# Inner feed-forward units: the low-part product of each weight tile right behind its high-part product

## The reference

```python
def swiglu(h, w_gate, w_up, w_down):
    return (jax.nn.silu(h @ w_gate) * (h @ w_up)) @ w_down
...
for i in range(DEPTH):
    g = norm_gain[i]
    h = swiglu(rmsnorm(x, g[0]), ffn_w_gate[i, 0], ffn_w_up[i, 0], ffn_w_down[i, 0])
    x = x + MACARON_WEIGHT * rmsnorm(h, g[1])
    ...
    h = swiglu(rmsnorm(x, g[4]), ffn_w_gate[i, 1], ffn_w_up[i, 1], ffn_w_down[i, 1])
    x = x + MACARON_WEIGHT * rmsnorm(h, g[5])
```

## Time and profile before

| | us |
|---|---|
| median of 3 runs (1092.91 to 1094.5) | 1093.01 |
| span of the profiled execution | 1091.1 |
| TensorE matmuls busy | 1081.5 (99%) |
| TensorE weight loads busy | 947.5 (87%) |
| VectorE busy | 810.8 (74%) |
| ScalarE busy | 662.7 (61%) |
| lines 1922 and 1928 busy | 287.9 and 160.7 |

### The profile page before, as it was taken

One profiled execution on the slowest core, in us unless ns is written; L12 is line 12 of the kernel. 1 busy time (PEld: TensorE's weight loads), 2 busy tenths in 40 slices (PEclk: granted clock), 3 DMA queues, 4 the chain that ended last, 5 costly groups with the idle time before them and its releaser, 6 DMA issues. The chain is left out here.

```text
span 1091.1 us, 17376 instructions
## 1 busy us (share of the span) xinstructions
PE 1081.5 (99%) x6271; PEld 947.5 (87%) x6271; DVE 810.8 (74%) x1230; ACT 662.7 (61%) x1002; POOL 64.0 (6%) x85
## 2 busy tenths in 40 slices
PE   9999999999999999999999999999999999999997
PEld 7888888899888888888888888899999988888886
DVE  5867666786688666668776667899999998766663
ACT  7555455784685455457554556687777797554552
POOL 3000000000010000000000000142111111000000
PEclk9999999999999999999999999999999999999999
DMA  9865645375356654555646534585544537656521
GB/s 285 307 225 165 208 155 153 102 234 187 118 184 234 217 192 156 191 193 184 223 161 222 189 119 135 184 268 186 176 154 154 167 116 237 223 165 230 173 96 39
DMA packets 162882, 199.29 MB, mean 183 GB/s; under 512 B 6373, under 2 KB 145857, under 8 KB 162833
## 3 DMA queue, kind: packets, MB, share of 16 engines
q1 hardware_dynamic: 160288, 190.86, 53.4%
q0 software_dynamic: 2384, 7.72, 2.0%
q10 hardware_dynamic: 160, 0.08, 0.0%
HBM read 197.56 MB, written 1.08 MB: 182 GB/s over the span
## 5 line engine op out<-in xcount | busy, mean ns | idle before, releaser
L1761 PE MATMUL ps<-ws,hT 128*128 128x512 f32 x1320 | 314.0, 392 | 0.0
L1211 DVE TENSOR_TENSOR ws<-raw,ws 128x1024 fp32r<-128x1024 f32 x180 | 218.4, 1223 | 108.1 <-ACT ws L657 108.1
L1922 PE MATMUL ps<-xT,ws 128*128 128x512 f32 x1152 | 287.9, 392 | 0.0
L1761 PEld LDWEIGHTS ps<-ws,hT 128*128 128x128 f32 x1320 | 243.9, 188 | 49.3 <-issue 1.1
L657 ACT ACTIVATE ws<-raw 128x1024 fp32r<-128x1024 f32 x183 | 191.5, 1057 | 148.8 <-PE ps L1928 121.2
L1922 PEld LDWEIGHTS ps<-xT,ws 128*128 128x128 f32 x1152 | 209.6, 189 | 38.8
L1118 DVE TENSOR_TENSOR ws<-raw,ws 128x2048 fp32r<-128x2048 f32 (+1 forms) x88 | 197.6, 2248 | 37.8 <-ACT ws L571 37.6
L1928 PEld LDWEIGHTS ps<-xT,ws 128*128 128x128 f32 x1152 | 157.2, 191 | 11.3
L571 ACT ACTIVATE ws<-raw 128x2048 fp32r<-128x2048 f32 x83 | 158.0, 1914 | 7.9 <-PE ps L1761 7.6
L1928 PE MATMUL ps<-xT,ws 128*128 128x256 f32 x1152 | 160.7, 283 | 0.0
L1815 PE MATMUL ps<-xT,ws 128*128 128x256 f32 x960 | 119.2, 284 | 0.0
(11 more groups left out here) (261 smaller groups left out, 896.5 us busy)
## 6 DMA issues: line engine op xcount, KB each, us to landing
raw<-in_ffn_w_down SPq DMA_DIRECT2D x88, 512.0 KB, 4.6
raw<-in_ffn_w_gate SPq DMA_DIRECT2D x86, 512.0 KB, 4.0
raw<-in_ffn_w_up SPq DMA_DIRECT2D x86, 512.0 KB, 5.0
raw<-in_ssd_w_in SPq DMA_DIRECT2D x48, 512.0 KB, 4.7
raw<-in_gla_w_in SPq DMA_DIRECT2D x24, 512.0 KB, 4.9
raw<-in_ssd_w_out SPq DMA_DIRECT2D x16, 512.0 KB, 4.5
raw<-in_gla_w_out SPq DMA_DIRECT2D x8, 512.0 KB, 5.1
exps<-cs_rows POOLq DMA_DIRECT2D x8, 512.0 KB, 4.9
```

What stands on the lines that cost most here:

```text
L1211: dve.tensor_tensor(ws[:, 0:2, 1, c], raw[:, 0:2, c], ws[:, 0:2, 0, c].bitcast(F32), ALU.subtract).then_inc(gu_lo, 1)
L1761: mm = pe.matmul(ps[:, 2 * t + n, :], hT[:, par, j, a, t * P:(t + 1) * P], ws[:, slot, b, off:off + 512], start=(first and j + a + b == 0) ...
L1922: pe.matmul(ps[:, A + 2 * s + j, :], weights(s, j, k, 0), xT[:, k, :, :].rearrange("p a n -> p (a n)"), start=(k == 0), stop=False, skip_g ...
```

## The change

`inner_sweep` waits for both the high and the low part at the start of a quarter. It then goes through s, j and k once: the wide matmul of a weight tile's high part, and directly behind it the narrow one of its low part. Before, all eight wide matmuls of the quarter came first, then the wait for the low part, then all eight narrow ones. The wait for the freed banks (`h_done`) stands in front of the first matmul of each s, and the signals `gu_read` and `gu_mm` are raised at the last matmul of the quarter and of each s of the last quarter, both as before.

```diff
@@ -1915,16 +1915,14 @@
                     for q in range(NQ):
                         ks = (2 * q, 2 * q + 1)
                         pe.wait_ge(gu_hi, unit * NQ + (q + 1))
-                        for s, j in itertools.product(range(2), range(2)):
-                            if q == 0 and j == 0 and not first:
+                        pe.wait_ge(gu_lo, unit * NQ + (q + 1))
+                        for s in range(2):
+                            if q == 0 and not first:
                                 pe.wait_ge(h_done, u * 2 + (2 * hiddens + s - 1))
-                            for k in ks:
+                            for j, k in itertools.product(range(2), ks):
                                 pe.matmul(ps[:, A + 2 * s + j, :], weights(s, j, k, 0),
                                           xT[:, k, :, :].rearrange("p a n -> p (a n)"), start=(k == 0), stop=False,
                                           skip_group_check=True)
-                        pe.wait_ge(gu_lo, unit * NQ + (q + 1))
-                        for s in range(2):
-                            for j, k in itertools.product(range(2), ks):
                                 mm = pe.matmul(ps[:, A + 2 * s + j, 0:T], weights(s, j, k, 1), xT[:, k, 0, :], start=False,
                                                stop=(k == KD - 1), skip_group_check=True)
                             if q == NQ - 1:
```

## The result

| | before | changed |
|---|---|---|
| median of the runs, us | 1093.01 | 1101.39 (1101.19 to 1101.71) |
| ratio, 95% interval | | 1.0075 [1.0064, 1.0086] |
| span of the profiled execution, us | 1091.1 | 1099.6 |

What follows compares the result with a forecast made beforehand. TensorE's own stream, busy 99% of the span, was taken as the bound. Losses of 2.3 + 2.2 + 0 = 4.5 us on the 1091.1 us span gave 1095.6, plus 1.9 to the median: 1097.5 us, range 1086 to 1102.

Steps and rivals of the forecast that it cites:

- the case of 353 ns a pair and over: Pace of a wide and narrow pair in the alternation: 353 ns or more, the slowest outcome, chance 0.18.
- the 2.81 called right: Quarters of a steady inner unit would take 2.81 us each if the forecast held.
- the 2.85 called wrong: A steady unit's quarter of 2.85 us would show the forecast wrong, as would 2.72.
- Term 1, the pace of a pair: All 1152 wide and narrow pairs in the feed-forward phases: 351 ns against 349 before, 2.3 us lost.
- 117 + 234 = 351 ns: A pair's price: narrow matmul halfway between its two paces, wide one as the first behind a narrow block.
- my upper end of 356: A pair's highest price: narrow at block pace 120, wide at 236 ns, the slowest following a narrow one; 8.1 us lost.
- the one with two transposes among wide matmuls: At a phase's end, six wide matmuls beside two transposes take 233 ns each, so a short interruption already costs 6 ns each.
- Term 2, the moved wait: First inner unit of each of four phases: weight load held back for the low part, 2.2 us lost; loop free.
- the estimates of 0.75, 0.6, 0.5 and 0.31: Microseconds by which the low part comes after the weight load's old start, in the four phases' first inner units.
- Term 3: Last quarter of a unit: gate half signalled 0.9 us sooner to ScalarE; TensorE does not wait for it, worth 0.
- The rival of the restored narrow matmul: Each of 1152 pairs at 340 ns, 10.4 us gained less 2.2, 1084.8 us; most of the 0.25 for faster.

Runs made afterwards that it cites:

- Groups of two: Two wide then two narrow matmuls in turn, with the early wait, against the kernel before: 1094.59 us, ratio 1.0009.
- runs of four: Four wide then four narrow matmuls in turn, with the early wait, against the kernel before: 1098.11 us, ratio 1.0047.

## Why the prediction was right

It said slower, 1097.5 us within 1086 to 1102; measured was 1101.4. The direction held, and both terms lie where they were said to lie. But the result is inside the range by only 0.6 us, and by the prediction's own signs it is the case of 353 ns a pair and over, which had a chance of 0.18: a quarter takes 2.83 us, halfway between the 2.81 called right and the 2.85 called wrong, and a unit 16.79 where 16.65 to 16.7 was called right. Half a microsecond of the 8.4 between the traces lies ahead of any changed instruction and has nothing to do with the reasoning.

- **Term 1, the pace of a pair,** was 2.3 us and is 6.1: 5.8 in the loop and, by the run with the wait taken back, some 0.3 in the four first units. The step was "117 + 234 = 351 ns". The 117 was right: narrow ones take 118, 120 and 113 in turn. The wide one takes 232, 241 and 236, 236.4 on average; I had taken 236 as the slowest that could follow a narrow one, and one in three is slower. That is 2.3 ns too little a pair, of which 0.5 is given back at the cheap start of a unit. The rest is a slip in the comparison: the 349 ns of before hold the down projection's loss, 24 ns a unit, and the 351 hold none, as if the alternation had none. It has more: the down projection takes 5.503 us against 5.467 at full resolution and 5.440 without loss. With it a pair costs (11.290 + 0.063)/32 = 354.8 ns, near my upper end of 356; the two misses together make 3.8 ns a pair. The row that pointed there was the one with two transposes among wide matmuls: a short interruption already brings nearly the whole loss, and I set the wide one at 234 all the same. Two readings from rounded rows were a little high: the first two wide matmuls behind narrow ones take 234 and 236 ns, not about 240, and the six behind two transposes 232, not 233.
- **The picture behind term 1** was a loss that each change back to wide sets off, and that fades over five wide matmuls. It is only in part borne out. Groups of two change back four times a quarter and lose less (16.59 us a unit) than blocks of eight, which change back once a quarter (16.61); and the alternation itself runs at 347 ns in some first units. That the time still fell inside the range owes something to luck.
- **Term 2, the moved wait,** was 2.2 us and is 1.8 in the change and 2.7 alone. It sits where it was said, and the steady loop's cover held. The four gaps alone come to 1.7 and 2.1 us above the normal ones; the estimates of 0.75, 0.6, 0.5 and 0.31 stand beside 0.74, 0.58, 0.46 and 0.30 in the kernel with the early wait alone. The 0.4 us between the gaps of the two kernels comes from the first phase, where the opening pair arrived later in the changed kernel's trace. Besides, the wider spacing behind the stall adds 0.4 us where the sweep is in blocks, and less than 0.2 in the alternation.
- **Term 3** was 0 and is 0: the chain came sooner by half a microsecond, and TensorE did not wait for it.
- **The rival of the restored narrow matmul** (340 ns a pair) is seen in one pair per unit of the changed kernel, the first. The Trainium skill's rule (TensorE: Matmul & The Clock Gate, section Back-to-back issue gap), by which the spacing in a stream of loads and matmuls is set by both together, was read in the prediction as giving this case. The loop doesn't show it, with 353 ns a pair. With the high part's tile cut to 32 columns it is seen in two stretches (340 and 341 ns), and there too the loop has 351.
- **The cause of the loss** is narrowed down, and stays open. Shown: it needs unequal widths beside each other (none with both 512 wide); it does not come from the bank, nor only from the room that a single load has (384 columns lose 9 to 10 ns a pair where 256 lose 13); 10 of its 13 ns go in the loop when both tiles are short; and the same stream of matmuls has more than one pace, by how it is entered. What in TensorE picks the pace, and why the loss is not monotonic in the length of the runs, I can't say from these runs.

## What to carry to other kernels

In a stream of matmuls that TensorE never waits in, the order of widths can itself be a cost. Here blocks of one kind that meet at the seams, or one block of each kind per unit, gained 0.1 to 0.15%, where strict alternation lost 0.6%. Between these ends it is not a matter of the number of changes (runs of four were worse than runs of two), so measure it, and measure the loop itself: the pace of the same matmuls behind a stall was another one. When a wait is moved ahead in a steady loop, look at the loop's first pass: its cover is missing there even where the loop has microseconds to spare.

## What the runs showed of the hardware that was not expected

- A strict alternation of 512 and 256 columns in float32r, with weight tiles of 128 columns, settled in all 32 units of the loop into a period of three pairs, 1060 ns: 232, 241 and 236 ns for the wide matmuls and 118, 120 and 113 for the narrow ones. Longer runs of wide matmuls come back to 226.7 from the sixth on.
- The same alternation has other patterns. Behind a stall it ran at 347 ns a pair in two of four first units and at 354 in the others; with the wide matmuls' tile cut to 32 columns it ran at 351 in the loop and at 340, the pace of the widths, in two stretches of the first units.
- At the widths' own pace 512 columns take 226.7 ns and 256 take 113.3, in proportion. A lone narrow matmul behind a long wide stream shows the 113; in a run of narrow ones all but the first two take 120.
- The width of a weight tile can count even where its load is hidden behind a wide matmul: cut from 128 to 32 columns there, with the output's partitions, the pair fell from 353 to 350 ns.
